# Where the four pairs of split weight buffers start in SBUF

## The reference

```python
def conformer_conv(h, w_in, b_in, dw, dw_b, ln_g, ln_b, w_out, b_out):
    u = h @ w_in + b_in                       # 2048 -> 4096
    ...
    return u @ w_out + b_out                  # 2048 -> 2048

def sq_relu_mlp(h, w1, w2):
    return jnp.square(jax.nn.relu(h @ w1)) @ w2      # 2048 -> 8192 -> 2048

def hybrid_mixer(...):
    proj = h @ w_in                           # 2048 -> 7184
    ...
    return o @ w_out                          # 2048 -> 2048

def conv_ffn(x, norm_g, w_gate, w_up, conv_w, conv_b, w_down):
    h = rmsnorm_2(x, norm_g)
    gate = causal_dwconv_2(h @ w_gate, conv_w) + conv_b
    return (jax.nn.silu(gate) * (h @ w_up)) @ w_down  # 2048 -> 5632 -> 2048
```

## Time and profile before

| | us |
|---|---|
| median of 3 runs | 2405.59 |
| lowest, highest | 2404.91, 2408.94 |
| the profiled run | 2405.66 |
| its span, first to last instruction | 2404.1 |

### The profile page before, as it was taken

One profiled execution on the slowest core, in us unless ns is written; L12 is line 12 of the kernel. 1 busy time (PEld: TensorE's weight loads), 2 busy tenths in 40 slices (PEclk: granted clock), 3 DMA queues, 4 the chain that ended last, 5 costly groups with the idle time before them and its releaser, 6 DMA issues.

```text
span 2404.1 us, 39484 instructions
## 1 busy us (share of the span) xinstructions
PE 2386.1 (99%) x16354; PEld 2126.8 (88%) x16354; DVE 1659.8 (69%) x2310; ACT 1106.3 (46%) x1496; POOL 59.8 (2%) x47
## 2 busy tenths in 40 slices
PE   9999999999999999999999999999999999999997
PEld 8888699888888888889998998999888888888886
DVE  5998856666666666678766455568776667667677
ACT  4000446544544544555636356556544434444444
POOL 0000000000000000000000000000100101000000
PEclk9999999999999999999999999999999999999999
DMA  7446456666666666655545455555666656666663
GB/s 246 154 146 208 140 192 185 188 190 192 191 185 194 190 190 189 192 184 170 158 125 141 124 159 160 176 179 162 194 190 187 190 186 191 188 189 191 187 192 123
DMA packets 379761, 427.96 MB, mean 178 GB/s; under 512 B 16536, under 2 KB 328128, under 8 KB 379584
## 3 DMA queue, kind: packets, MB, share of 16 engines
q1 hardware_dynamic: 374464, 421.58, 57.1%
q10 hardware_dynamic: 5120, 3.86, 0.5%
HBM read 423.27 MB, written 3.67 MB: 178 GB/s over the span
## 4 chain that ended last, share of the span: by engine, by line
PE 95%; DVE 2%; ACT 1%; DMA 1%; issue 0%; SPq 0%; ACTq 0%; DVEq 0%
PE product L607 39%; PE product L556 21%; PE product L609 20%; PE product L581 9%; PE product L578 1%; DMA w_raw<-in_cc_w_in 0%; DVE x_residual L664 0%; DMA x_residual<-in_x 0%; DVE scratch L742 0%; DVE w_lo L515 0%; PE small L1754 0%; PE small L1729 0%; PE small L1689 0%; PE small L1465 0%; PE small L2149 0%
## 5 line engine op out<-in xcount | busy, mean ns | idle before, releaser
L515 DVE TENSOR_TENSOR w_lo<-w_raw,w_hi 128x1024 fp32r<-128x1024 f32 x708 | 868.9, 1230 | 526.1 <-ACT w_hi L508 525.0
L508 ACT ACTIVATE w_hi<-w_raw 128x1024 fp32r<-128x1024 f32 x708 | 747.3, 1058 | 815.7 <-PE product L609 578.9
L607 PE MATMUL product<-h_operand,w_hi 128*128 128x512 f32 x2496 | 867.4, 392 | 0.0
L609 PE MATMUL product<-h_operand,w_lo 128*128 128x256 f32 x2496 | 700.1, 280 | 0.0
L607 PEld LDWEIGHTS product<-h_operand,w_hi 128*128 128x128 f32 x2496 | 467.5, 187 | 101.6
L609 PEld LDWEIGHTS product<-h_operand,w_lo 128*128 128x128 f32 x2496 | 473.1, 190 | 0.1
L607 PE MATMUL product<-mlp_hidden,w_hi 128*128 128x512 f32 x1024 | 355.3, 391 | 0.0
L609 PE MATMUL product<-mlp_hidden,w_lo 128*128 128x256 f32 x1024 | 287.2, 280 | 0.0
L607 PE MATMUL product<-mid_operand,w_hi 128*128 128x512 f32 x704 | 248.9, 397 | 0.0
L556 PE MATMUL product<-h_operand,w_hi 128*128 128x256 f32 x1280 | 237.8, 287 | 0.3 <-DVE w_lo L515 0.3
L607 PEld LDWEIGHTS product<-mlp_hidden,w_hi 128*128 128x128 f32 x1024 | 191.7, 187 | 41.6
(11 more groups left out here) (325 smaller groups left out, 2214.6 us busy)
## 6 DMA issues: line engine op xcount, KB each, us to landing
w_raw<-in_mlp_w SPq DMA_DIRECT2D x256, 512.0 KB, 3.9
w_raw<-in_w_in SPq DMA_DIRECT2D x112, 512.0 KB, 3.7
w_raw<-in_w_gate SPq DMA_DIRECT2D x88, 512.0 KB, 3.5
w_raw<-in_w_up SPq DMA_DIRECT2D x88, 512.0 KB, 3.9
w_raw<-in_w_down SPq DMA_DIRECT2D x88, 512.0 KB, 4.4
w_raw<-in_cc_w_in SPq DMA_DIRECT2D x128, 256.0 KB, 2.9
w_raw<-in_w_out SPq DMA_DIRECT2D x32, 512.0 KB, 4.1
w_raw<-in_cc_w_out SPq DMA_DIRECT2D x28, 512.0 KB, 4.6
```

The source lines that it names most:

```text
L508: act.activation(k.w_hi[i % SPLIT], raw_of(k, i), ACT.Copy).then_inc(*k.act_done.mark("w_hi", i))
L515: dve.tensor_tensor(k.w_lo[i % SPLIT], raw_of(k, i), k.w_hi[i % SPLIT].bitcast(F32), ALU.subtract).then_inc(*k.dve_done.mark("w_lo", i))
L607: pe.matmul(out, hi[:, kk, n], x.both[:, kt].rearrange("p a t -> p (a t)"), start=s == 0 and kk == 0, stop=False, skip_group_check=True)
L609: done = pe.matmul(out[:, 0:T], lo[:, kk, n], x.hi[:, kt, :], start=False, stop=last and kk == WIDE_K - 1, skip_group_check=True)
```

## The change

Each of the eight split buffers becomes the tail of a block that is wider by 0 to 64 floats in front: `BELOW_HI` and `BELOW_LO` give that width for w_hi and w_lo (and for w_first, which lies over w_lo). Nothing else in the program changes.

```diff
@@ -239,6 +239,8 @@
 WARM = 5
+BELOW_HI = (0, 8, 56, 0)
+BELOW_LO = (64, 8, 56, 64)
 WIDE_K = SLOT_K * COLS // PAIR
@@ -293,10 +295,13 @@
-        self.w_hi = [self.sbuf(f"w_hi{i}", [P, SLOT_K, COLS], F32R) for i in range(SPLIT)]
+        slot = lambda name, i, pad, dt, stack=None: self.sbuf(f"{name}{i}", [P, pad + SLOT_K * COLS], dt, stack)[:, pad:].rearrange(
+            "p (k n) -> p k n", n=COLS)
+        self.w_hi = [slot("w_hi", i, BELOW_HI[i], F32R) for i in range(SPLIT)]
         with ExitStack() as early:
-            self.w_first = [self.sbuf(f"w_first{i}", [P, SLOT_K, COLS], F32, early) for i in range(SPLIT)]
-        self.w_lo = [self.sbuf(f"w_lo{i}", [P, SLOT_K, COLS], F32R) for i in range(SPLIT)]
+            self.w_first = [slot("w_first", i, BELOW_LO[i], F32, early) for i in range(SPLIT)]
+        self.w_lo = [slot("w_lo", i, BELOW_LO[i], F32R) for i in range(SPLIT)]
+        self.sbuf("above_weights", [P, 1024 - sum(BELOW_HI) - sum(BELOW_LO)])
```

## The result

| | before | after |
|---|---|---|
| median of the runs, us | 2405.25 (4 runs) | 2426.60 (4 runs) |
| lowest, highest | 2404.91, 2408.94 | 2424.97, 2428.01 |
| span of the profiled run | 2404.1 | 2425.1 |

The ratio is 1.0088, with a 95% interval of 1.0075 to 1.0102: slower by 21 us, where 7 were forecast and 2424 was the upper end of the range.

The account below looks back on a forecast made before the run. The prediction took TensorE's matmul-to-matmul intervals as the bound. Its terms, +5.8, +2.0, +0.7, -2.0 and +0.7 us, summed to +7.2 on 2405.59, giving 2412.8 us, range 2393 to 2424.

Parts of the forecast that it names:

- TensorE's intervals are the time, the rest has cover: Whole kernel: only matmul-to-matmul intervals count; ScalarE's and VectorE's splits have 579 and 525 us of waiting as slack.
- The price of a distance of 32, 6.6 ns a pair: Buffer 1's wide pairs pay mid_operand's extra over mlp_hidden, 353.6 - 347.0 ns: 880 pairs, +5.8 us.
- no effect: Rival, 22%: the 6.6 ns belongs to mid_operand's own misalignment, weights can move freely, time stays at 2405.6.
- Buffer 0 stays: Buffer 0 keeps its place, so its wide matmuls stay at 392 and 280 ns; no cost.
- Buffer 2 at 256: Wide pairs of buffer 2 at distance 256: half of 4.5 ns a pair, 2.2 ns x 880 = +2.0 us.
- buffer 3: w_hi at 256, w_lo at 0: only the load beside the 256-column matmul changes, +0.7 us on 880 pairs.
- The rival that priced 256 like 32: Rival, 10%: buffer 2's distance of 256 costs what 32 does, +3.9 us more, 2417.
- faster: Rival, 18%: equal places collide and 256 bytes separates the streams; buffer 2 pairs gain 8 ns, together -10.7 us, 2395.0.
- slower still: Rival, 8%: any distance other than 0 costs like mid_operand's slow half, +28 us, 2434; sign: L607 mean above 396.
- Narrow products: 256-column matmuls on h_operand in buffers 1 to 3: 119.9 to 118.3 ns, -2.0 us; bounds -6 and +3 ns each.
- cc_w_out: Its narrow products go to the mixed-place price, above today's: 512 x 1.3 ns = +0.7 us.
- In every fourth slot the 512-column matmul on h_operand alternates: Sign of being right: L607 there alternates between about 391 and 401 ns, as on mid_operand.

Follow-up runs that it names:

- all_32: All eight split buffers start 32 bytes later than in the kernel before; 2424.2 us, ratio 1.0054.
- all_64: All eight split buffers at place 64 (address modulo 512), against the kernel before; 2417.7 us in one run.
- b1_32: Only buffer 1, its w_hi and w_lo, moved to place 32, against the kernel before; 2427.2 us, ratio 1.0093.
- one_slot: Kernel before with slot 301 alone, one of 708, written to and read from an address 32 bytes further; 2412.0 us, ratio 1.0005.
- b2_256: Only buffer 2, w_hi and w_lo, moved to place 256, against the kernel before; 2407.9 us, ratio 1.0010.
- all_256: All eight split buffers start 256 bytes later than in the kernel before; 2407.7 us, ratio 1.0005.
- lo_512: All four w_lo buffers start 512 bytes later than in the kernel before, w_hi where it was; 2406.0 us, ratio 1.0002.
- b1lo_32: Only w_lo of buffer 1 moved to place 32, against the kernel before; 2407.4 us, ratio 1.0000.

## Why the prediction was wrong

The direction was right, and the size was off by a factor of three. Step by step:

- *TensorE's intervals are the time, the rest has cover.* Right: the splits kept their durations and their slack, and TensorE's longest wait is 1.6 us (1.5 before).
- *The price of a distance of 32, 6.6 ns a pair.* Right: all_32 has 353.6 ns on mlp_hidden, in the alternation of mid_operand. The rival "no effect", by which the 6.6 ns belonged to mid_operand's own misalignment, falls with it, and with all_64, where mid_operand is as misaligned as before and takes 347.0 ns. The Trainium skill (SBUF — State Buffer, section "Who interferes with whom") calls TensorE's two read ports independent. The measurement decides against reading this as "the addresses do not matter to each other": 347.0 and 353.6 ns for the same instructions, by the distance of their addresses. Whether the ports do it or something behind them, no run shows.
- *"Buffer 0 stays", and each buffer pays for its own place.* This is the step that failed. The sum gave buffer 1 880 pairs x 6.6 ns = 5.8 us. b1_32 shows 21 us for it, since the other 2,640 pairs left the interval of 346.7 ns too, at unchanged addresses (modulo 4096), and one_slot shows how: the rhythm outlasts the slot that tips it. The term was read as a function of address, and it has a memory.
- *Buffer 2 at 256, +2.0 us; buffer 3, +0.7.* 256 shows no cost clear of the noise (b2_256, all_256; 347.0 ns a pair on mlp_hidden); of the two sides that the sum halved, "a shift by 256 may cost nothing" was the right one. The rival that priced 256 like 32 is out, and so is "faster", by which a pair at 256 should have gained 8 ns, and so is "slower still" as a mechanism, though its 2434 was the closest of the slower ones and its sign, a mean of the 512-column matmul above 396 ns, came true with 398: not every distance is dear.
- *Narrow products.* -2.0 us on h_operand was forecast, and the chain's 96 give 1,920 x (119.3 - 119.9) = -1.2; cc_w_out +1.0 where +0.7 was forecast. The bound of -6 ns was reached and just passed (119.9 to 113.5 on h_operand), but at a distance of 64, which in the change only buffer 1 has, on mid_operand.
- *"In every fourth slot the 512-column matmul on h_operand alternates".* Seen, in buffer 1 of b1_32 above. The other half of the sign, that buffer 0 stays at 392 and 280, failed: the buffers that did not move turn in threes at 353 ns.

The hint was there. The trace before showed mid_operand's products and h_operand's in turn in the FFN, each with its own interval, and I took this for proof that a pair answers to its own addresses. That all rows at distance 0 give 390 to 392 ns was read from the row of mlp_hidden; the row of h_operand in the earlier trace rows reaches 586, and among its pairs are the 64 in the slow rhythm (two windows of 32, mean 398 and 399 ns). Nor does a change of operand begin the rhythm anew by rule: in one_slot it goes on through three, and in lo_512 the h_operand products between two on mid_operand, at distance 0 as before, take 353 ns in one turn and 347 in the next. The windows' view of its L613:

```profile
1832.00:1920.00 88.00, 88.00 (x250) 46.79 (x249) 1.00 0.62 187
1967.00:2053.00 86.00, 86.00 (x249) 46.38 (x248) 1.00 0.63 190
```

What stays open: what inside the chip holds the rhythm, and what decides when it is entered and left; why w_hi and w_lo of buffer 1 must both be off for the full loss; why a mix of 0, 96 and 256 costs some 6 us. In several kernels the executions fall into groups some 10 us apart (b1lo_32: six from 2405.1 to 2407.5, four from 2415.2 to 2417.8), and the kernel before is one of them. A rhythm that comes out one way or the other would explain it, but no two executions of one kernel were profiled, so this was not shown. Distances of 192 and 224 were not tried.

## What to carry to other kernels

Where TensorE is the bound, read the interval from start to start of one form of matmul (busy time by count) for each moving operand: if the same form has two values, look at the addresses of the weights and of the moving operand modulo 256. Give all buffers of a ring the same place, since one that differs (by 32 or 64 bytes here) can slow all of them, and choose the distance by the width of the moving operand (here 96 bytes for pairs of 512 and 256 columns, 64 for 256 columns alone; distance 0 worked but could be tipped). A price found on one operand holds for a whole layout only if a kernel with just one buffer moved gives its share of it.

## What the runs showed of the hardware

- For float32r matmuls with one load of 128 x 128 weights each, the interval goes with the distance between the two read addresses: 347.0, 353.6, 353.6, 347.0 and 351.4 ns a pair at 0, 32, 64, 96 and 128; 120.0, 113.4 and 117.4 ns for 256 columns alone at 0, 64 and 96. It is the same again 256 bytes further for 0 and 32, the two that were tried. The Trainium skill, TensorE: Matmul & The Clock Gate, section "Back-to-back issue gap", has 518 and 262 cycles for an isolated matmul of 512 and of 256 columns; as an estimate that is 325 ns a pair at 2.4 GHz. No run reached it; with the granted clock at 1.00 the least was 347.
- At distance 0 there are two rhythms with the same code and addresses, 346.6 and 352.9 ns in one execution of one_slot and 346.9 and 353 in the kernel before, and a single slot of eight pairs 32 bytes off was followed by the slow one for at least 170 us.
- Splits on ScalarE and VectorE that write to or read from the shifted buffers keep their durations within 3 ns: 1058 and 1230 in the changed kernel as before, 1061 and 1229 with all eight buffers 32 bytes off.
